# One DRAM store of a bias line becomes a short store and eight DRAM-to-DRAM copies

## The chip, the cores and the metric

The kernel runs on one core of a Trainium2 chip. The metric is the device time of one execution, in microseconds (us). The engines of the core are TensorE (PE; its weight loads PEld), VectorE (DVE), ScalarE (ACT), GpSimd (POOL) and SyncE (SP), which only issues transfers here. Transfers issued by SP and by ACT run on the same 16 DMA engines.

## What is computed

One step of a two-layer network over 576 tokens (512 of a prompt, 64 of a decoding request) with 1024 features. Layer 0 is a matrix-memory mixer and a gated FFN, layer 1 a differential attention with shared keys and values and a gated FFN. The change concerns the relative-position bias of the attention, which depends only on the distance between key and query:

```python
def _diff_attention(xm, k_all, v_all, q_offset, ...):
    table = rel_bias.astype(jnp.float32)          # 32 buckets x 8 heads
    def block(args):
        s = jnp.einsum('bqhcd,bkhcd->bhcqk', qblk, k_all)
        bias = table[_rel_bucket(k_pos[None, :] - q_pos[:, None])]
        p = jax.nn.softmax(jnp.where(mask, s + bias, NEG_BIG), axis=-1)
        a = p[:, :, 0] - lam * p[:, :, 1]
        return jnp.einsum('bhqk,bkhe->bqhe', a, v_all)
```

Because of that dependence, one line of 704 values for each head holds every bias that is needed: key minus query from -575 to 128. A tile of biases is a set of shifted windows of that line, one shift for each query.

## The kernel before, in words

The activations lie feature by token, 8 tiles of 128 features by 576 tokens. Every weight matrix is cut into units: a unit is 128x1024 values (512 KB), or 128x1408 for the down projections of the FFN. All projections are made in three matmuls each, with weights and activations split into a high and a low part. One unit goes through a fixed pipeline:

- SP loads it into `raw[u % 2]` (`load_unit`, L326 to L331). Before that it waits until POOL has split unit u-2 (`lo_split`).
- POOL makes `w_hi` and `w_lo` from it (`split_unit`, L408 to L418). It waits for the load and until TensorE has finished unit u-2 (`unit_done`).
- TensorE multiplies with it (`project`, L474 to L488: 8 k-tiles by 3 products by 2 halves of the tokens, 48 matmuls; `project_values`, L512 to L536: 30 matmuls of 512 columns a unit).

Beside the units SP loads tiles of the modulation weights, `ada_ring` (`load_ada`, L333 to L337, also 512 KB), which TensorE uses after a unit (L490 to L500). All of SP's loads go through one queue, q1 in the profile, in the order in which the code lists them. ACT's stores go through another, q10.

The order of units is: unit 0 the mixer's gates, 1 to 4 its queries, 5 to 8 its keys, 9 to 16 its values, then the rest of layer 0; 93 to 100 (`U_AK`) are the attention's keys, 101 to 108 (`U_AV`) its values, 109 to 116 its queries, 117 on (`U_AO`) its output projection. SP's loads for units 93 to 120 are the loop at L390 to L395; two tiles of `ada_ring` are loaded in it after units 94 and 96 (`KQ_ADA`, L83).

The bias line is made early. TensorE multiplies the bias table by one-hot columns (L562 to L566), VectorE copies the result to `line_sb`, 8 partitions by 704 values, and ACT stores it to DRAM (L996 and L997) as soon as it has prepared the first activations. The store writes the line of each head 128 times, so that DRAM holds 8 x 128 x 704 values. In layer 1, `load_head(h)` (L374 to L388) reads it back with a row step of LINE - 1, one value less than a row: row p of the tile is the line shifted by p. That gives `bias_p` (128 rows of 512 values) and `bias_s` (twice 64 rows of 576 values). `load_head(0)` is issued behind unit 117 and waits for the store (L378).

```python
sa.dma_start(line_dram, line_sb[:, :].unsqueeze(1).broadcast_to([H, P, LINE])).then_inc(line_stored, 16)   # L997
sp.wait_ge(line_stored, 16)                                                                                # L378
```

Of the kernel before, what the change touches and what calls it, by code (L numbers as in the profile page):

```python
# [37 lines left out]
P = 128  # L38
# [8 lines left out]
H = 8  # L47
# [7 lines left out]
LINE = 704  # L55
# [6 lines left out]
U_AK = U_FFN0 + 2 * FFN_HALF  # L62
U_AV, U_AQ, U_AO = U_AK + 8, U_AK + 16, U_AK + 24
# [8 lines left out]
def is_down(u):  # L72
    return any(d <= u < d + KT for d in down_units())


def stream_index(u):

    d = sum(1 for v in range(u) if is_down(v))
    return d if is_down(u) else u - d
# [41 lines left out]
def loop(eng, count, body, steps=None, per_turn=0):  # L121

    if count == 1:
        body(0)
        return
    start = steps.n if steps else 0
    with eng.Fori(0, count) as i:
        if steps:
            steps.turns = i * per_turn
        body(i)  # L130
    if steps:
        assert steps.n - start == per_turn, (steps.n - start, per_turn)
        steps.n, steps.turns = start + per_turn * count, 0


def build(nc, x_in, cond, consts, small, oh_line, table, w_stream, w_down, ada_w, c0n_in, kcache, vcache,
          line_dram, y_out, cp_out, cs_out, m_out, k_out, vp_out, vs_out):
    with ExitStack() as ctx:
        sem = lambda name: ctx.enter_context(nc.semaphore(name))
# [6 lines left out]
        def at(name, shape, offset, dt=F32):  # L146
            return nc.alloc_sbuf_tensor_at(name, shape, dt, offset=offset)
# [35 lines left out]
        line_sb = at("line_sb", [H, LINE], arena + 8 * T * 4)  # L183
# [51 lines left out]

        cond_ready, params_ready, x_ready, line_in = sem("cond_ready"), sem("params_ready"), sem("x_ready"), sem("line_in")
        line_stored, line_done, line_mm = sem("line_stored"), sem("line_done"), sem("line_mm")
        ada_first_in = [sem(f"ada_first_in{g}") for g in range(ADA_START // 2)]
        ada_in = [sem(f"ada_in{s}") for s in range(2)]
        ada_row_mm, ada_row_ready, xm_ready = (sem(n) for n in ("ada_row_mm", "ada_row_ready", "xm_ready"))  # L240
# [83 lines left out]
        @block.sync  # L324
        def _(sp):
            def load_unit(u0, i=0):  # L326

                src, blocks = (w_down, FH) if is_down(u0) else (w_stream, KT)
                if u0 >= 2:
                    sp.wait_ge(lo_split, i * 2 + (u0 - 1))  # L330
                sp.dma_start(raw[:, u0 % 2, 0:blocks * P], src[i * 2 + stream_index(u0)]).then_inc(raw_in[u0 % 2], 16)  # L331

            def load_ada(n0, i=0):  # L333

                if n0 >= ADA_START + 2:
                    sp.wait_ge(ada_mv, i * 2 + (n0 - ADA_START - 1))
                sp.dma_start(ada_ring[:, n0 % 2].rearrange("p k c -> p (k c)"), ada_w[i * 2 + n0]).then_inc(ada_in[n0 % 2], 16)  # L337

            def load_pairs(u0, pairs, ada0=None):

                def pair(i):
                    for j in range(2):
                        load_unit(u0 + j, i)
                        if ada0 is not None:
                            load_ada(ada0 + j, i)
                loop(sp, pairs, pair)

            sp.dma_start(cs_in, cond).then_inc(cond_ready, 16)
            for g in range(ADA_START // 2):
                dst = ada_first[0][:, 2 * g:2 * g + 2] if g < 6 else ada_first[1][:, 2 * g - 12:2 * g - 10]  # L350
                sp.dma_start(dst.rearrange("p u k c -> p u (k c)"),
                             ada_w[2 * g:2 * g + 2].rearrange("u p n -> p u n")).then_inc(ada_first_in[g], 16)
                if g == 1:
                    sp.dma_start(x[:, :, :], x_in).then_inc(x_ready, 16)
                    for c0, c1 in ((C_ID, C_MEAN + 1), (C_BLK, C_HEAD), (C_OHC, NCONST)):
                        sp.dma_start(cst[:, c0:c1], consts[:, c0:c1]).then_inc(params_ready, 16)
                    sp.dma_start(sml[:, :], small).then_inc(params_ready, 16)
            load_unit(0)
            load_unit(1)
            sp.dma_start(oh_sb[:, :], oh_line).then_inc(line_in, 16)  # L360
            sp.dma_start(tab_sb[:, :], table).then_inc(line_in, 16)
            sp.dma_start(c0n[:, :, :], c0n_in).then_inc(c0n_loaded, 16)
            load_ada(16)
            load_ada(17)
            for u in (2, 3, 4):
                load_unit(u)
            load_pairs(5, 25, 18)
            load_pairs(55, 1, 68)
            load_pairs(57, 3)
            load_pairs(63, 11, 70)  # L370
            load_pairs(85, 4)


            def load_head(h):  # L374
                s = h % 2
                if h == 0:
                    sp.wait_ge(ada_done, ADA_UNITS)
                    sp.wait_ge(line_stored, 16)  # L378
                elif h == 1:
                    sp.wait_ge(unit_done, U_AO)  # L380
                else:
                    sp.wait_ge(av_done, 5 * (h - 1))
                sp.dma_start(bias_p[s][:, :], bass.AP(line_dram.tensor, h * P * LINE + 191, [[LINE - 1, P], [1, 512]])).then_inc(stream_in[s], 16)
                for c in range(2):
                    sp.dma_start(bias_s[c * TS:(c + 1) * TS, s],
                                 bass.AP(line_dram.tensor, h * P * LINE + 63, [[LINE - 1, TS], [1, T]])).then_inc(stream_in[s], 16)
                sp.dma_start(kc_sb[s][:, :], kcache[h]).then_inc(stream_in[s], 16)
                sp.dma_start(vc_sb[s][:, :, :].rearrange("p k e -> p (k e)"), vcache[h]).then_inc(stream_in[s], 16)  # L388

            for u in range(U_AK, U_AO + 4):  # L390
                load_unit(u)
                if u in KQ_ADA:
                    load_ada(92 + KQ_ADA.index(u))
                if u == U_AO:
                    load_head(0)  # L395
            for h in range(1, H):
                load_head(h)
            load_pairs(U_AO + 4, 2)
            for hf in range(2):
                load_pairs(U_FFN1 + hf * FFN_HALF, FH)  # L400
                load_pairs(U_FFN1 + hf * FFN_HALF + 2 * FH, KT // 2)
# [531 lines left out]
        def _(sa):  # L933
# [60 lines left out]
                sa.wait_ge(xm_ready, m + 1)  # L994
                af(act[0][0][:, m, 0:T], xr[:, m, :], ACT.Copy).then_inc(hi_ready[A_IN], 1)
            sa.wait_ge(line_done, 2)  # L996
            sa.dma_start(line_dram, line_sb[:, :].unsqueeze(1).broadcast_to([H, P, LINE])).then_inc(line_stored, 16)  # L997


            sa.wait_ge(unit_done, 1)  # L1000
# [9 lines left out]
            for m in range(8):  # L1010
                u = U_Q + m
# [86 lines left out]
            for h in range(H):  # L1098
                u = U_O + h
# [790 lines left out]
```

## Time and profile before

| | |
|---|---|
| median of 3 runs | 1737.95 us (1737.13 to 1746.68) |
| the profiled execution | 1734.42 us, of it 1732.6 us in the span |
| mean granted TensorE clock | 0.972 |
| TensorE busy | 1639.4 us, 95% of the span |
| POOL, VectorE, ScalarE busy | 43%, 42%, 20% |
| q1, SP's loads | 46112 packets, 165.55 MB, 28.8% of 16 engines' span |
| q10, ACT's stores | 2728 packets, 10.49 MB, 2.5% |

The profile shows one execution. Busy times are shares of the whole span, so they hide short stretches in which another engine sets the pace; these are found in the views by window. The share of a DMA queue is the time that its packets took, as a share of the time of all 16 DMA engines.

### The profile page before, as it was taken

The numbers are of one execution on the slowest core, as the hardware profiler recorded it, in microseconds if no ns is written. First come the engines' busy times: TensorE is split into PE (matmuls) and PEld (weight loads), VectorE is DVE, ScalarE is ACT, GpSimd is POOL, SyncE is SP. The second block draws the span as 40 slices with busy tenths as digits, with TensorE's granted clock in tenths as the row PEclk, the third lists the DMA queues.
The fourth block names the chain that finished last, engine by engine and source line by source line (L and its number), as shares of the span: only waits on it lengthen the run. The fifth ranks groups of instructions, "written<-read, shape, count | busy, mean of one in ns | idle before, by whom it ended". The sixth has DMA issues, their size and how long they took to land.

```text
span 1732.6 us, 31223 instructions
## 1 busy us (share of the span) xinstructions
PE 1639.4 (95%) x12009; PEld 1479.1 (85%) x12009; DVE 719.1 (42%) x1230; ACT 354.8 (20%) x796; POOL 751.6 (43%) x436
## 2 busy tenths in 40 slices
PE   5789999999999999999999999788899999999999
PEld 2678733789999999999998879565799999999999
DVE  3400244545433321333586515678544443134431
ACT  2201034212211100111122112367521110001100
POOL 2534300234444554444554444224255555555563
PEclk8889999999999999999999999799899999999999
DMA  8364200234444422444322125222022222222231
GB/s 334 71 160 136 98 13 1 74 121 135 136 144 145 150 78 100 146 145 145 106 88 74 61 73 207 87 63 66 23 73 82 77 85 100 70 73 85 89 105 67
DMA packets 48908, 176.99 MB, mean 102 GB/s; under 512 B 5544, under 2 KB 5928, under 8 KB 48456
## 3 DMA queue, kind: packets, MB, share of 16 engines
q1 hardware_dynamic: 46112, 165.55, 28.8%
q10 hardware_dynamic: 2728, 10.49, 2.5%
q8 instruction: 47, 0.77, 0.2%
q14 instruction: 21, 0.17, 0.0%
HBM read 165.53 MB, written 10.49 MB: 102 GB/s over the span
## 4 chain that ended last, share of the span: by engine, by line
PE 83%; DVE 4%; DMA 3%; issue 2%; ACT 2%; POOL 1%; DVEq 0%; ACTq 0%; SPq 0%; POOLq 0%
PE psum L485 61%; PE psum L532 7%; PE psum L494 2%; DMA raw<-in_w_stream 2%; PE psum L653 1%; DMA ada_ring<-in_ada_w 1%; PE psum L635 1%; PE psum L654 1%; PE psum L876 1%; DVE act_lo L1368 1%; PE psum L919 1%; PE psum L779 1%; PE psum L863 1%; PE psum L505 1%; POOL w_lo L418 1%
## 5 line engine op out<-in xcount | busy, mean ns | idle before, releaser
L416 POOL TENSOR_SCALAR w_hi<-raw 128x1024 fp32r<-128x1024 f32 (+1 forms) x185 | 205.6, 1112 | 860.1 <-PE psum L485 672.7
L485 PE MATMUL psum<-act_hi,w_hi 128*128 128x288 f32 x2160 | 479.4, 303 | 19.9 <-POOL w_lo L418 10.6
L418 POOL TENSOR_TENSOR w_lo<-raw,w_hi 128x1024 fp32r<-128x1024 f32 (+1 forms) x185 | 487.8, 2637 | 15.4
L485 PE MATMUL psum<-act_lo,w_hi 128*128 128x288 f32 x2160 | 469.4, 299 | 0.0
L485 PE MATMUL psum<-act_hi,w_lo 128*128 128x288 f32 x2160 | 468.6, 298 | 0.0
L485 PEld LDWEIGHTS psum<-act_hi,w_hi 128*128 128x128 f32 x2160 | 351.7, 191 | 38.9 <-issue 31.2
L485 PEld LDWEIGHTS psum<-act_hi,w_lo 128*128 128x128 f32 x2160 | 353.1, 191 | 0.0
L485 PEld LDWEIGHTS psum<-act_lo,w_hi 128*128 128x128 f32 x2160 | 353.1, 191 | 0.0
L485 PE MATMUL psum<-hid_hi,w_hi 128*128 128x288 f32 x704 | 151.1, 296 | 0.0
L485 PE MATMUL psum<-hid_hi,w_lo 128*128 128x288 f32 x704 | 150.8, 296 | 0.0
L485 PE MATMUL psum<-hid_lo,w_hi 128*128 128x288 f32 x704 | 150.8, 296 | 0.0
L1411 DVE SCALAR_TENSOR_TENSOR tmp<-tmp,tiny 128x512 f32<-128x512 f32 x88 | 142.5, 1658 | 6.0 <-ACT tmp L1139 1.0
L1384 DVE SCALAR_TENSOR_TENSOR x<-psum,mod,x 128x288 f32 x144 | 51.2, 410 | 198.2 <-PE psum L485 194.5
L485 PEld LDWEIGHTS psum<-hid_hi,w_hi 128*128 128x128 f32 x704 | 113.4, 189 | 0.6 <-issue 0.6
L485 PEld LDWEIGHTS psum<-hid_hi,w_lo 128*128 128x128 f32 x704 | 113.5, 189 | 0.0
L485 PEld LDWEIGHTS psum<-hid_lo,w_hi 128*128 128x128 f32 x704 | 113.4, 189 | 0.0
L1406 DVE COPY tiny<-psum 128x2 f32<-128x2 f32 x44 | 7.0, 159 | 254.3 <-PE psum L485 254.3
L977 ACT ACTIVATE sml<-psum 128x128 f32<-128x128 f32 x80 | 22.3, 278 | 369.3 <-PE psum L494 368.9
L1145 ACT ACTIVATE hid_hi<-tmp 128x576 f32 (+1 forms) x44 | 30.2, 686 | 261.7 <-DVE tmp L1411 261.7
L1139 ACT ACTIVATE tmp<-tmp,tiny 128x512 f32<-128x512 f32 x88 | 42.3, 529 | 123.2 <-DVE tmp L1402 123.1
L532 PE MATMUL psum<-w_hi,act_hi 128*128 128x512 f32 x160 | 63.9, 399 | 3.8 <-DVE kf L1650 1.6
L532 PE MATMUL psum<-w_lo,act_hi 128*128 128x512 f32 x160 | 63.1, 395 | 0.0
(255 smaller groups left out, 1769.7 us busy)
## 6 DMA issues: line engine op xcount, KB each, us to landing
raw<-in_w_stream SPq DMA_DIRECT2D x153, 512.0 KB, 3.3
ada_ring<-in_ada_w SPq DMA_DIRECT2D x80, 512.0 KB, 3.3
raw<-in_w_down SPq DMA_DIRECT2D x32, 704.0 KB, 4.0
ada_first<-in_ada_w SPq DMA_DIRECT2D x8, 1024.0 KB, 15.2
line<-line_sb ACTq DMA_DIRECT2D x1, 2816.0 KB
x<-in_x SPq DMA_DIRECT2D x1, 2304.0 KB, 12.2
out_k<-kt_sb ACTq DMA_DIRECT2D x1, 2304.0 KB, 8.4
bias_s<-line SPq DMA_DIRECT2D x16, 144.0 KB, 3.4
```

The source lines that it names most:

```text
L416: pool.tensor_scalar(hi, src, 1.0, 0.0, ALU.mult, ALU.add).then_inc(hi_split, 1)
L418: pool.tensor_tensor(lo, src, hi.bitcast(F32), ALU.subtract).then_inc(lo_split, 1)
L485: last = mm(psum[:, 2 * s + half, 0:n_cols], w_parts[s][wp][:, k, :], parts[ap][:, k, half * HT:half * HT + n_cols], start=(k == 0 and n = ...
L494: last = mm(out(slice(32 * j, 32 * j + 32)), cs_col(2 * j + kk), w(2 * j + kk), start=(kk == 0), stop=(kk == 1))
L505: mm(psum[:, 5, bass.ds(i * 4 + 2 * n0, 2)], row_sb[:, n0 % 2, :], ada_sel, start=True, stop=True).then_inc(ada_done, 1)
L532: last = mm(psum[:, tt, :], parts[ap][:, k, t0:t0 + P], w, start=(k == 0 and n == 0), stop=(k == KT - 1 and n == 2))
L635: mm(psum[:, g % 2, 0:TP - j * P], k[:, j * P:(j + 1) * P], q[:, j * P:TP], start=True, stop=True).then_inc(s_ready, 1)
L977: af(row_sb[:, s, :], psum[:, row_bank(n0), 0:P], ACT.Copy).then_inc(row_ready, 1)
L1139: last = af(tmp[:, 4, a0:a1], tmp[:, 2, a0:a1], ACT.Silu, bias=shift_sb[:, 0, g:g + 1])
L1145: af(hid[0][:, i, :], tmp[:, 5, :], ACT.Copy).then_inc(hhi_ready, 1)
L1384: last = stt(out=xs, in0=psum[:, 2 * s + half, a0:a1], scalar=mod[:, i * 2 + (8 * c + j), g:g + 1], in1=xs, op0=ALU.mult, op1=ALU.add)
L1411: last = stt(out=tmp[:, 5, a0:a1], in0=tmp[:, 3, a0:a1], scalar=shift_sb[:, 1, g:g + 1], in1=tmp[:, 4, a0:a1], op0=ALU.add, op1=ALU.mult)
```

## The change

ACT stores only one row for each head (8 rows of 704 values). SP gets eight new transfers, one for each head, in the loop over the attention's units: `spread_line(h)` is issued right after the load of unit 93 + h, ahead of an `ada_ring` load where there is one. It copies row 0 of the head's block in DRAM to the block's rows 1 to 127. The first of them waits for ACT's store. `load_head(0)` waits for all eight.

```diff
+        line_spread = sem("line_spread")
...
                 if h == 0:
                     sp.wait_ge(ada_done, ADA_UNITS)
-                    sp.wait_ge(line_stored, 16)
+                    sp.wait_ge(line_spread, 16 * H)
...
+            def spread_line(h):
+
+                if h == 0:
+                    sp.wait_ge(line_stored, 16)
+                sp.dma_start(line_dram[h, 1:P, :], line_dram[h, 0:1, :].broadcast_to([P - 1, LINE])).then_inc(line_spread, 16)
+
             for u in range(U_AK, U_AO + 4):
                 load_unit(u)
+                if u < U_AV:
+                    spread_line(u - U_AK)
                 if u in KQ_ADA:
                     load_ada(92 + KQ_ADA.index(u))
...
             sa.wait_ge(line_done, 2)
-            sa.dma_start(line_dram, line_sb[:, :].unsqueeze(1).broadcast_to([H, P, LINE])).then_inc(line_stored, 16)
+            sa.dma_start(line_dram[:, 0, :], line_sb[:, :]).then_inc(line_stored, 16)
```

## Rows read from the trace of the kernel before

**Rows 1.** The page: busy time, share and instructions; the chain that ended last.

```profile
PE 1639.4 (95%) x12009; PEld 1479.1 (85%) x12009; DVE 719.1 (42%) x1230; ACT 354.8 (20%) x796; POOL 751.6 (43%) x436
...
PE 83%; DVE 4%; DMA 3%; issue 2%; ACT 2%; POOL 1%; DVEq 0%; ACTq 0%; SPq 0%; POOLq 0%
```

**Rows 2.** Busy time by stretch: window, us, busy (instructions), clock, DMA share, GB/s.

```profile
60.00:80.00 20.00, 19.48 (x170) 18.83 (x168) 10.26 (x9) 6.64 (x10) 6.66 (x4) 1.00 0.62 99
80.00:100.00 20.00, 13.71 (x101) 13.43 (x101) 0.00 (x0) 0.93 (x2) 6.80 (x4) 0.83 0.63 121
100.00:120.00 20.00, 11.41 (x100) 10.74 (x98) 0.00 (x0) 1.46 (x3) 6.82 (x4) 0.83 0.63 154
120.00:140.00 20.00, 19.86 (x161) 18.37 (x156) 1.01 (x8) 3.27 (x9) 10.32 (x6) 1.00 0.56 182
```

**Rows 3.** The waits from 79 to 135 us: total us, times, longest.

```profile
POOL w_hi L416 <- DMA raw<-in_w_stream: 36.7, 5, 16.3
...
PE psum L494 <- DMA ada_ring<-in_ada_w: 8.6, 1, 8.6
...
PE psum L485 <- POOL w_lo L418: 6.8, 1, 6.8
```

**Rows 4.** The chain, 78 to 136 us: start, duration, what.

```profile
110.72 1.08 PE psum L494 x16
111.80 7.63 PE psum L485 x48
...
120.12 6.60 PE psum L485 x48
...
127.41 6.60 PE psum L485 x48
134.01 0.02 issue
134.03 0.66 ACT qk L1013
```

**Rows 5.** TensorE's timeline, end of unit 3 and start of unit 4.

```profile
79.19 0.29 PE L494 MATMUL psum<-ada_ring,cst 128*32 128x128 f32 x3
...
86.27 0.84 PE L485 MATMUL psum<-act_hi,w_hi 128*128 128x288 f32 x2 [6.79 <-POOL w_lo L418]
```

**Rows 6.** Queue q10 from 66.5 to 69.5 us: packets, MB, share of 16 engines.

```profile
q10 hardware_dynamic: 56, 0.16, 48.5%
```

**Rows 7.** Median us to landing of a unit's load, 60 to 100 us; the whole span.

```profile
raw<-in_w_stream SPq DMA_DIRECT2D x4, 512.0 KB, 20.0
...
raw<-in_w_stream SPq DMA_DIRECT2D x153, 512.0 KB, 3.3
```

**Rows 8.** Queue q1 from 940 to 950 us, where one 512 KB load runs.

```profile
DMA packets 144, 0.52 MB, mean 52 GB/s; under 512 B 16, under 2 KB 16, under 8 KB 144
...
q1 hardware_dynamic: 144, 0.52, 16.7%
```

**Rows 9.** SP's timeline, 881 to 925 us: the last is the load of unit 97.

```profile
889.91 9.12 SPq L331 DMA_DIRECT2D raw<-in_w_stream  x2
899.07 0.43 SPq L337 DMA_DIRECT2D ada_ring<-in_ada_w  x1
...
924.90 0.33 SPq L331 DMA_DIRECT2D raw<-in_w_stream  x1
```

**Rows 10.** The chain in the key projection: units 97, 98; the first values unit.

```profile
946.56 6.42 PE psum L485 x48
...
953.96 6.42 PE psum L485 x48
...
977.75 7.42 PE psum L532 x31
```

**Rows 11.** POOL's timeline, the split of unit 97.

```profile
938.40 1.05 POOL L416 TENSOR_SCALAR w_hi<-raw 128x1024 fp32r<-128x1024 f32 x1 [3.87 <-PE psum L485]
939.53 2.40 POOL L418 TENSOR_TENSOR w_lo<-raw,w_hi 128x1024 fp32r<-128x1024 f32 x1
```

**Rows 12.** Queue q1, 1111 to 1119 us; queue q10, 1060 to 1070 us.

```profile
q1 hardware_dynamic: 736, 1.61, 68.8%
...
q10 hardware_dynamic: 263, 2.78, 66.0%
```

**Rows 13.** The page's DMA issues: the store that is changed.

```profile
line<-line_sb ACTq DMA_DIRECT2D x1, 2816.0 KB
```

## Prediction

> **What bounds the kernel now.** I read the page first: TensorE is busy for 95% of the span and makes 83% of the chain that ended last [rows 1]. So a change to transfers pays only where TensorE waits for one, and costs only where it makes TensorE wait. Next I read the busy time by stretch around the store of the bias line, which ACT issues at about 58.6 us. From 60 to 80 us TensorE is busy, from 80 to 120 us it is busy for 25.1 of 40 us while the DMA engines are busy for 0.63 of the time at a modest rate, from 120 us it is busy again [rows 2]. The waits say what was late: POOL waited 36.7 us for units, TensorE 8.6 us for an `ada_ring` tile and 6.8 us for a split that POOL began late [rows 3]. Then I looked at the store by itself. From 66.5 to 69.5 us only its queue runs: 56 packets in 3 us, 48.5% of 16 engines, so 7.8 engines busy; 0.485 x 16 x 3 / 56 = 0.416 us for a packet of 2816 B [rows 6]. The store has 8 rows (the heads) as its outermost count, and it keeps 8 engines busy. It holds 8 x 128 packets, 128 for each engine, 53 us of work at that pace. Beside it a unit's load lands after 20.0 us instead of 3.3 [rows 7], because half of its packets go through the eight engines that the store keeps busy.
>
> **Part 1: the store shrinks from 2816 KB [rows 13] to 22.5 KB.** Eight packets take the place of 1024, so units 4 to 8 should arrive as later units do. Unit 3 with its modulation ends at 79.48 us [rows 5]. Undisturbed, a unit costs 7.29 us from start to start (120.12 to 127.41) and 6.60 us alone [rows 4]. Units 4 to 8 then end at 79.48 + 4 x 7.29 + 6.60 = 115.2 us; they ended at 134.0. **Gain: 18.8 us.** The waits give the same: 6.8 + 8.6 us, and the slow restarts behind them, in which the clock fell to the lower of its two levels, 1.2 GHz, for a few us (granted 0.83 on average in these stretches [rows 2]), account for the other 3.4. What is late next is nothing: from 120 us on, with the same loads and no store, TensorE is at 19.86 of 20 us. ACT's issue of the store sits ahead of the gates' evacuation, but TensorE does not wait for that from 60 to 80 us, so I count nothing for it.
>
> **Part 2: eight copies in q1 beside units 93 to 100.** Each is 127 rows of 2816 B, 357.6 KB, and 127 packets. The question that decides the case is on how many engines they run. A load of 128 rows makes 144 packets, 9 for each engine, one of them small [rows 8]; the store of 8 rows kept 8 engines busy. Every transfer seen is dealt out in equal shares of its outermost count. 127 is a prime number: equal shares leave **one engine with all 127 packets**. The Trainium skill says this outright: in "DMA: Bandwidth & Descriptors", section "Why a DMA increments its semaphore by 16 and not by 1", the number of engines is the largest up to 16 that divides the outermost count on both sides, and 127 partitions run on one. By that rule the sum is the one below; the trace agrees for 8 and 128, and has no odd count to show.
>
> *One copy on one engine.* No row shows a DRAM-to-DRAM packet. The nearest rows that read DRAM in rows of this size are the head loads (2048 and 2304 B rows): 0.688 x 16 x 8 us = 88.1 engine-us for 1.61 MB, 18.3 GB/s for an engine [rows 12]. That gives 0.154 us a packet and **C = 19.6 us** a copy, which I take: both ends are in DRAM, and rows of 2 to 3 KB are the right size. The low bound is ACT's large stores to DRAM, 0.66 x 16 x 10 = 105.6 engine-us for 2.78 MB, 26.3 GB/s, C = 13.6 [rows 12]. The high bound is the store's own 0.416 us, C = 52.8 [rows 6]; it reads the same few partitions over and over, which the copy does not, so I think it far off. The same page, in "Latency and other measured facts", has 207 GB/s each way for copies between DRAM tensors on all engines; as an estimate that is 12.9 GB/s an engine, C = 27.6, and by it the execution would take 1873 us.
>
> *What waits behind them.* A unit's load has 8 packets and a small one on that same engine, in the same queue and in order, and its wait in POOL is for all of it. A load of 512 KB takes 0.167 x 10 = 1.67 us of each engine [rows 8]. The load of unit 93 is issued at 889.91 us [rows 9] and takes 3.3 us [rows 7], so the first copy starts at 893.2. Until unit 101 has landed, the engine must do 8 copies, 8 loads (units 94 to 101) and 2 `ada_ring` tiles. With C at 13.6 or above it is never empty: unit 97 was requested at 924.90 us [rows 9], when the engine would already be four requests behind. So unit 101 lands at 893.2 + 10 x 1.67 + 8C = 909.9 + 8C. POOL splits it in 3.5 us [rows 11], and TensorE starts it at 913.4 + 8C. It started at 977.75 [rows 10]. With 1.5 us for one slow restart (the second one of part 1: 7.63 + 1.08 us where the usual is 6.60 and about 0.6 [rows 4]) the delay is 8C - 62.9 us. **Loss: 156.8 - 62.9 = 93.9 us.** The 62.9 us are the cover: between unit 97 and unit 98 TensorE works 7.4 us [rows 10] and an engine needs only 1.67 of them for a load, and a load is some 10 us early for POOL (unit 97: 924.90 + 3.3 against a split that begins at 938.40 [rows 11]). With C at 19.6 a unit takes 21 us instead of 7.4.
>
> SP is in order, so an issue of a copy stands ahead of the next load; but the next load waits for POOL anyway, and the time is below the spare. The wait of the first copy for `line_stored` costs nothing: that store is over by some 800 us. The wait in `load_head(0)` now is for the copies, which end ahead of unit 101's load, over 100 us before it. The amount that is read back is the same. Nothing later gives the delay back, since all stages behind hang on TensorE.
>
> **Sum.** Against the profiled execution: 1734.4 - 18.8 + 93.9 = 1809.5 us. That execution is 3.5 us under the median of the runs shown, so **1813 us**. By C = 13.6: 1734.4 - 18.8 + 45.9 = 1761.5, or 1765 as a median. By C = 52.8: 1734.4 - 18.8 + 359.5 = 2075.
>
> **Rivals.**
> - *The copies run on all 16 engines* (shares rounded up, 8 packets for each engine, 1.2 us at 0.154). For it: no row shows a count that doesn't divide. Against it: both counts that rows show went in equal shares. Then a load lands at most 1.2 us later, with 10 us spare, and only part 1 is left: 1734.4 - 18.8 = 1715.6, as a median **1719 us**, faster. Chance 0.12. Seen from the price, it decides below C = 10.2 us (8C = 62.9 + 18.8), 0.080 us a packet; on one engine that is 35 GB/s, which no row reaches (chance 0.02, about no change).
> - *The copies crawl*: one engine, and a packet costs more than 0.24 us, because each reads the same 2816 B again and writes DRAM behind it. For it: the store, which also reads the same source over and over, took 0.416 us. Against it: the head loads. From 1900 to 2075 us. Chance 0.08.
> - *The front doesn't speed up*: the loads of units 4 to 8 were late for another reason. Against it: a queue with 48.5% of the engines in the very stretch [rows 6]. Then 1813 + 19 = 1832 us. Chance 0.03.
>
> **The numbers.** The forecast, one engine at 0.107 to 0.24 us a packet, has 0.75. That and the third rival lie in 1765 to 1900, about 0.78. I keep the range there: the fast case at 1719 and the slow tail are what it leaves out. A measurement of this kernel tells about 0.5%, 9 us, from no change. Faster 0.12, within it 0.02, slower 0.86.
>
> **What would show it.** Right: from 80 to 120 us TensorE busy all through and units landing after 3.3 us; from about 930 to 1070 us TensorE in bursts of 6.4 us at intervals of 21, POOL waiting for `raw`, DMA engines busy for little more than a sixteenth of the time, the copies about 20 us or more from issue to landing, the first values unit starting near 1050 us (977.75 - 18.8 + 93.9). Wrong: the copies landing within some 4 us and the key projection as before (the first rival); intervals above 32 us (the second); 20 us landings before 120 us (the third).

## The result and the profile after

The changed kernel takes 1763.62 us (1763.06 to 1766.38, 4 runs) against 1737.62 us (1737.13 to 1746.68, 4 runs): 1.014 times as long, 95% interval 1.0106 to 1.0175. It is slower, as forecast, but by 26 us and not by 75; that is just below the range. The profiled execution took 1763.78 us, 29.4 more than the one of before.

**The front.** The view by stretch, with the columns of [rows 2], and the landing of a unit's load from 60 to 100 us:

```profile
80.00:100.00 20.00, 20.00 (x174) 19.54 (x174) 0.00 (x0) 2.05 (x5) 9.67 (x6) 1.00 0.47 151
100.00:120.00 20.00, 19.86 (x174) 18.50 (x173) 1.01 (x8) 3.80 (x9) 10.32 (x6) 1.00 0.40 137
```

```profile
raw<-in_w_stream SPq DMA_DIRECT2D x6, 512.0 KB, 3.3
```

TensorE works for 39.86 of 40 us where it worked for 25.1 [rows 2], and a load lands after 3.3 us where it took 20.0 [rows 7]. The first matmul of the mixer's core starts at 200.0 us and no longer at 218.4: 18.4 us gained, 18.8 forecast.

**The key projection.** The queue from 963 to 970 us, when only a copy runs:

```profile
q1 hardware_dynamic: 65, 0.18, 6.5%
```

6.5% of 16 engines is 1.04 engines: one engine carries the copy. 65 packets in 7 us are 0.108 us for each. The forecast had 0.154. POOL's timeline, its splits of units 96 and 98 to 100 (the `ada_ring` tile behind unit 96's copy makes the step at unit 97, not shown, 1.3 us longer):

```profile
925.22 1.04 POOL L425 TENSOR_SCALAR w_hi<-raw 128x1024 fp32r<-128x1024 f32 x1 [10.80 <-DMA raw<-in_w_stream]
...
956.50 1.58 POOL L425 TENSOR_SCALAR w_hi<-raw 128x1024 fp32r<-128x1024 f32 x1 [10.95 <-DMA raw<-in_w_stream]
...
971.47 1.05 POOL L425 TENSOR_SCALAR w_hi<-raw 128x1024 fp32r<-128x1024 f32 x1 [10.60 <-DMA raw<-in_w_stream]
...
986.47 1.04 POOL L425 TENSOR_SCALAR w_hi<-raw 128x1024 fp32r<-128x1024 f32 x1 [10.96 <-DMA raw<-in_w_stream]
```

Units come 15.0 us apart, where TensorE needs 7.4. SP's timeline in the same stretch, the load of unit 98, its copy, the load of unit 99:

```profile
930.69 14.22 SPq L332 DMA_DIRECT2D raw<-in_w_stream  x1
944.95 0.86 SPq L395 DMA_DIRECT2D line<-line  x1
945.85 13.95 SPq L332 DMA_DIRECT2D raw<-in_w_stream  x1
```

The issue of a load is itself held for 14 us while the engine that carries the copies is behind. That engine is called engine 0 below; the views don't number the engines. The first matmul of the attention's scores starts at 1135.7 us and not at 1105.6. From the 10 small matmuls behind unit 93 (L815, now L824) to there it takes 227.6 us and not 182.5: the copies cost 45.1 us. They were to cost 93.9.

The rest of the account: of the 18.4 us of the front 15.0 are left when unit 93 ends. The mixer's core took 89.1 us from its first to its last score matmul where it took 85.9; TensorE's granted clock was 0.92 in that stretch where it was 0.96. The kernel below that keeps the long store has 89.3 there too, so the short store is not what lengthens it. -15.0 + 45.1 = 30.1, and 29.4 remain at the end.

### The profile page after: what moved, and what is told of

Its sections match the earlier page's. It is cut to its first block, busy times and chain, and to the rows that moved or that the text cites. A ratio compares the mean times of both kernels' runs of the same rounds, so it can differ in the third digit from the quotient of the medians.

```text
span 1762.0 us, 31231 instructions
## 1 busy us (share of the span) xinstructions
PE 1647.7 (94%) x12009; PEld 1484.5 (84%) x12009; DVE 735.9 (42%) x1230; ACT 354.9 (20%) x796; POOL 756.3 (43%) x436
## 4 chain that ended last, share of the span: by engine, by line
PE 84%; DMA 3%; SPq 3%; ACT 2%; DVE 2%; POOL 2%; issue 1%; POOLq 0%; DVEq 0%; ACTq 0%
PE psum L494 63%; PE psum L541 7%; DMA raw<-in_w_stream 3%; PE psum L503 3%; SPq L332 2%; PE psum L662 1%; PE psum L644 1%; PE psum L663 1%; SPq L338 1%; PE psum L885 1%; PE psum L928 1%; POOL w_lo L427 1%; PE psum L872 1%; PE psum L514 1%; PE psum L900 1%
## 5 line engine op out<-in xcount | busy, mean ns | idle before, releaser
L541 PE MATMUL psum<-w_hi,act_lo 128*128 128x512 f32 x160 | 64.0, 400 | 0.0
```

The lines of the kernel that those rows point to most:

```text
L541: last = mm(psum[:, tt, :], parts[ap][:, k, t0:t0 + P], w, start=(k == 0 and n == 0), stop=(k == KT - 1 and n == 2))
```

## The experiments

Theory 1: a DMA is dealt out in equal shares of its outermost count, so 127 rows stand on one engine, and each load in the same queue waits behind them there. Theory 2: SP's issue of the copies costs the time. Theory 3: the bytes of the copies disturb the loads. "Keys" below is the time from the end of unit 93 to the first score matmul (182.5 us before, 227.6 in the changed kernel). All kernels start from the changed one. Where the number of copies or stores differs, the counts that are waited for are changed with it; the cuts of the code leave that out, and `...` stands for the rest of a line.

**rows112_15.** 112 + 15 rows.

```diff
-                sp.dma_start(line_dram[h, 1:P, :], ...broadcast_to([P - 1, LINE])).then_inc(line_spread, 16)
+                for r0, r1 in ((1, 113), (113, P)):
+                    sp.dma_start(line_dram[h, r0:r1, :], ...broadcast_to([r1 - r0, LINE])).then_inc(line_spread, 16)
```

> Each head's copy is cut into two: 112 rows and 15 rows. Theory 1 (equal shares of the rows; a load stands behind the copy on engine 0): 7 packets on each of 16 engines and 1 on each of 15, under 1 us beside each load, no wait for a unit in the key projection. Only the gain of the short store is left: 1738 - 19 = 1719 us. Theory 2 (SP's issue of the copies is what costs, whatever the engines): 16 issues in place of 8, the key projection as slow as in the changed kernel or slower, 1764 us or more. Theory 3 (the DRAM traffic of the copies disturbs the loads): the same bytes, 1764 us.

Measured: 1722.65 us, ratio 0.9897 (0.9861 to 0.9934). In the key projection POOL waits for no load any more, only for TensorE:

```profile
POOL w_hi L426 <- PE psum L495: 58.5, 13, 9.9
```

Keys: 185.5 us. The same bytes, issued by the same SP in twice the number of issues, cost at most 3 us. Even these are not the issues: rows125_2 below has as many and takes 182.2 us. TensorE is busy in all of the first 20 us of this stretch in both, but with a granted clock of 0.82 here and 1.00 there. Theories 2 and 3 are out.

**rows97_30 and rows67_60.** The same edit with the cut at row 98 or at row 68.

> Each head's copy is cut into 97 rows (a prime, one engine) and 30 rows (15 engines, 2 packets each). Theory 1, set to the changed kernel (0.111 us a packet, delay 46.6 us at 127 packets): 8 x (30 x 0.111 - 0.22) = 25 us less on engine 0, delay 22 us, so 1738 - 19 + 22 = 1741 us. Units land about 11.9 us apart (15.0 in the changed kernel). Theories 2 and 3: 1764 us or more.

Measured: 1737.91 us, ratio 0.9993 (0.9975 to 1.0012). Its POOL timeline:

```profile
954.84 1.04 POOL L426 TENSOR_SCALAR w_hi<-raw 128x1024 fp32r<-128x1024 f32 x1 [8.10 <-DMA raw<-in_w_stream]
966.77 1.04 POOL L426 TENSOR_SCALAR w_hi<-raw 128x1024 fp32r<-128x1024 f32 x1 [8.46 <-DMA raw<-in_w_stream]
978.78 1.04 POOL L426 TENSOR_SCALAR w_hi<-raw 128x1024 fp32r<-128x1024 f32 x1 [8.09 <-DMA raw<-in_w_stream]
```

Units come 12.0 us apart. Engine 0 has 97 + 2 packets for each and not 127: 28 packets less for 3.0 us less, so 0.107 us a packet and 15.0 - 127 x 0.107 = 1.4 us for a load. Keys: 202.0 us, 19.5 over before; 22 were expected.

> Each head's copy is cut into 67 rows (a prime, one engine) and 60 rows (15 engines, 4 packets each). Theory 1: engine 0 needs 67 x 0.111 + 0.44 + about 1 for the load = 8.9 us a unit against the 7.4 of TensorE; 8 x 1.5 = 12 us are lost, which the early start of the loads (11 to 15 us) covers. Delay 0 to 2 us, so 1719 to 1721 us, though one engine still carries half of every copy. Theories 2 and 3: 1764 us or more.

Measured: 1719.54 us, ratio 0.9898 (0.986 to 0.9936), keys 182.7 us. One engine still carries 67 + 4 of the 127 packets of each copy, and nothing waits. What counts is only whether the busiest engine keeps up long enough: 127, 99 and 71 packets cost 45.1, 19.5 and 0.2 us.

**rows125_2.** The cut at row 126.

> Each head's copy is cut into 125 rows and 2 rows. Equal shares: 125 = 5 x 25, five engines with 25 packets (2.7 us), two with 1. While only a copy runs, 5 of 16 engines are busy, a share of 0.31, and the key projection doesn't wait. If shares were rounded (or one engine taken for every odd count), the share would be 1.0 for 0.9 us, or 0.06 for 14 us.

One execution took 1723.41 us. The queue from 884 to 886 us:

```profile
q1 hardware_dynamic: 88, 0.25, 31.8%
```

0.318 x 16 = 5.1 engines for 125 = 5 x 25 rows, at 0.114 us a packet. Shares are equal, and the largest divisor up to 16 decides: 5 of 125, 1 of 127. It is one execution, so only the count of engines is read from it, not its time.

**every_third.** The copies behind units 93, 96, ... 114.

```diff
-                if u < U_AV:
-                    spread_line(u - U_AK)
+                if u < U_AO and (u - U_AK) % 3 == 0:
+                    spread_line((u - U_AK) // 3)
```

> The eight copies keep their 127 rows and their queue, but stand behind every third unit (93, 96, ... 114), through the key, value and query projections. Theory 1: engine 0 needs 14 us for a copy and 3 x 1.3 us for the loads in the 22 us that TensorE takes for three units, and the one load behind a copy is late by less than its 15 us of cover. No delay, 1719 us, with one engine still carrying every copy. If a copy on one engine cost its own time wherever it stands, the delay would be that of the changed kernel, 1764 us.

Measured: 1730.85 us, ratio 0.9954 (0.9931 to 0.9977), keys 194.8 us: 12 us of loss, none expected. POOL's timeline, the split of unit 114 and of unit 115:

```profile
1062.13 1.05 POOL L425 TENSOR_SCALAR w_hi<-raw 128x1024 fp32r<-128x1024 f32 x1 [10.15 <-DMA raw<-in_w_stream]
...
1077.38 1.05 POOL L425 TENSOR_SCALAR w_hi<-raw 128x1024 fp32r<-128x1024 f32 x1 [11.77 <-DMA raw<-in_w_stream]
```

The first seven copies are hidden: TensorE never waits for a split before 1055 us. The eighth stands behind unit 114. SP's timeline there, an `ada_ring` tile, the load of unit 114, the copy, the load of unit 115:

```profile
1057.32 0.33 SPq L338 DMA_DIRECT2D ada_ring<-in_ada_w  x1
1057.69 0.47 SPq L332 DMA_DIRECT2D raw<-in_w_stream  x1
1058.20 0.58 SPq L395 DMA_DIRECT2D line<-line  x1
1058.82 6.39 SPq L332 DMA_DIRECT2D raw<-in_w_stream  x1
```

`KQ_ADA` has four entries and not only the two named in the description of the kernel: tiles are loaded after units 94, 96, 112 and 113. SP is in order, and the last tile waited 14.9 us for TensorE to be done with an older one, with unit 114's load behind it. That load was late before the change too (issued at 1067.80 us, 0.37 us after the tile; POOL waited 10.2 us). So this copy starts with no cover left: unit 115's load lands 18.4 us after its issue, and TensorE waits 8.0 us for the splits where it waited 0.8. These are 7 of the 12 us. The rest is a lower granted clock at both ends, 0.85 in the first 20 us of the stretch (1.00 before) and 0.89 from 1055 to 1105 us (0.97 for the same work before). The theory stands; the expectation took the cover to be the same everywhere.

**act_queue.** The same 127-row copies, issued by ACT in its own stream, one with every second unit of the mixer's projections.

```diff
+                if m % 2 == 1:
+                    spread_line(m // 2)
...
+                    if n == 1:
+                        spread_line(4 + 2 * nh)
...
+                spread_line(5 + 2 * nh)
```

> The eight 127-row copies, unchanged in shape, are issued by ACT in its own queue, one with every second unit of the mixer's query, key and value projections (every 15 us). Theory 1 in its strict form (what costs is the order within SP's queue, not the engine's load): engine 0 takes turns between the two queues, a unit's load lands 1 to 3 us later than 3.3 us, no wait, 1719 us. If the engine's total work were the cause: each pair of units puts 14.1 us of copy and some 4 us of loads on engine 0 in 15 us, 8 x 3 = 24 us less the cover, 1725 to 1735 us.

Measured: 1736.68 us, ratio 0.9975 (0.9957 to 0.9993), nearly 18 us above the 1719 that theory 1 gave and within 2 us of the 1725 to 1735 of its rival. Keys: 184.5 us. Where the copies run, a unit's load lands after 6.0 us (median from 60 to 200 us) and not 3.3, and from 60 to 120 us TensorE waits for none: in another queue a long copy delays the loads on its engine by 3 us and does not block them. But from 120 to 140 us TensorE is busy for 11.08 of 20 us. ACT's timeline says why:

```profile
116.01 7.46 ACTq L1004 DMA_DIRECT2D line<-line  x1
...
123.55 16.16 ACTq L1030 DMA_DIRECT2D out_m<-rows  x1
```

ACT itself was held for 24 us at issuing, as SP is in the changed kernel, and ACT has evacuations to do. TensorE waited for them:

```profile
PE psum L507 <- ACT sml L979: 9.8, 1, 9.8
```

A third hold of 6.1 us follows at 192 us, and TensorE waits 3.4 us behind it. These two waits are 13 us; the slower clock around them (granted 0.83 from 140 to 160 us, 0.86 from 180 to 200) is the likely rest, not taken apart. The rival expectation, engine 0's total work, is not what delays: no unit was late. But that work, 13.7 us for a copy and the loads beside it every 15 us, may be what held ACT.

**old_store_and_copies.** The long store kept, with the copies.

```diff
-            sa.dma_start(line_dram[:, 0, :], line_sb[:, :]).then_inc(line_stored, 16)
+            sa.dma_start(line_dram, line_sb[:, :].unsqueeze(1).broadcast_to([H, P, LINE])).then_inc(line_stored, 16)
```

> The long store of before is kept beside the new copies, which write the same values again: part 2 of the change without part 1. Expected are the front as before and the key projection as in the changed kernel: 1738 + 46.6 = 1785 us. If the short store gained nothing, it would be the changed kernel's 1764.

Measured: 1784.0 us, ratio 1.0267 (1.0216 to 1.0318). Keys: 228 us. The front is as before (TensorE busy for 25.4 of 40 us) and the keys are as in the changed kernel, so the two parts of the change add up: 1784.0 - 1763.6 = 20.4 us are what the short store gains.

**unaligned.** The reads start 4 bytes further.

```diff
-                sp.dma_start(line_dram[h, 1:P, :], line_dram[h, 0:1, :]...
+                sp.dma_start(line_dram[h, 1:P, 0:LINE - 1], line_dram[h, 0:1, 1:LINE]...
```

> Each copy reads its row from the second value on, at an address 4 bytes further, and writes 703 values (the biases are shifted by one place: this part of the result is changed). It asks why the head loads, whose rows start at every 4-byte step, moved 18.3 GB/s an engine and misled the forecast, while the copies move 26. If the start address is the cause, a packet costs 0.154 us and units land 20.9 us apart: 8 x 5.9 = 47 us more, 1811 us. If one more piece of 256 B is read for each packet, 12 in place of 11: units 16.2 us apart, about 1773 us. If the address does not matter: 1764 us.

Measured: 1763.59 us, ratio 1.015 (1.0098 to 1.0201). Units come 14.98 us apart, as in the changed kernel. A start 4 bytes on costs nothing here. The dearer case of the expectation, one more piece of 256 B, was not made: the read is 4 bytes shorter as well and ends where the row ends, so with a row that starts on a boundary of 256 B it touches the same 11 pieces.

**half_packets.**

```diff
+                for c0 in (0, LINE // 2):
+                    sp.dma_start(line_dram[h, 1:P, c0:c0 + LINE // 2], ...
```

> Each copy is cut by columns into two of 127 packets of 1408 B, both on one engine: the same bytes in twice the packets. If the cost goes by bytes (26 GB/s): units land 15.0 us apart as in the changed kernel, 1764 us. If a packet has a fixed part of 0.02 us: 17.5 us apart, 1784 us. If the shorter rows of the head loads (2048 and 2304 B) explain their slower pace, the fixed part must be about 0.15 us: over 30 us apart, 1880 us or more.

Measured: 1771.85 us, ratio 1.02 (1.0148 to 1.0253). Units come 16.2 us apart (979.75 to 995.91 in POOL's timeline): 127 packets more for 1.2 us, a fixed part of 0.009 us. Shorter rows explain little of the head loads' pace.

**one_copy.** One copy for all heads, behind unit 93's load.

```diff
-                sp.dma_start(line_dram[h, 1:P, :], line_dram[h, 0:1, :].broadcast_to([P - 1, LINE])).then_inc(line_spread, 16)
+                sp.dma_start(line_dram[:, 1:P, :], line_dram[:, 0:1, :].broadcast_to([H, P - 1, LINE])).then_inc(line_spread, 16)
...
-                if u < U_AV:
+                if u == U_AK:
```

> One copy for all heads (8 x 127 rows) behind unit 93's load, in place of eight. Equal shares of its outermost count, 8, put 127 packets on each of 8 engines, as the old store had 128. If a packet between two DRAM places costs the 0.108 us of the changed kernel on all 8 engines, they are busy for 14 us once, one load is late by less than its 15 us of cover, and only part 1 is left: 1719 us. If 8 engines at once make the packets as slow as the old store's (0.416 us), they are busy for 53 us: 53 - 15 = 38 us late, 1757 us.

Measured: 1720.86 us, ratio 0.9892 (0.9864 to 0.992). The queue from 882 to 885 us:

```profile
q1 hardware_dynamic: 211, 0.59, 51.3%
```

Eight engines at 8 x 3 / 211 = 0.114 us a packet, 198 GB/s, where the old store had eight engines at 0.416 us. So neither the number of engines nor writing to DRAM made that store slow. Keys: 182.7 us, nothing lost.

**store_four_heads.** Heads 0 to 3 by the long store, the others by copies of 112 and 15 rows.

```diff
+            sa.dma_start(line_dram[4:H, 0, :], line_sb[4:H, :]).then_inc(line_stored, 16)
+            sa.dma_start(line_dram[0:4], line_sb[0:4, :].unsqueeze(1).broadcast_to([4, P, LINE])).then_inc(line_stored, 16)
```

> It asks what made a packet of the old store cost 0.416 us. ACT stores the lines of heads 0 to 3 128 times as before, from 4 partitions and on 4 engines; heads 4 to 7 get one row and copies of 112 and 15 rows. If reading from a few partitions is the limit (the 8 partitions gave 52.6 GB/s in all), 4 partitions give half of it, a packet stays at about 0.42 us, 4 engines are held for 53 us, and the front is as slow as before: 1738 us. If the 8 engines slowed each other elsewhere, a packet falls to about 0.21 us, 27 us, and some 14 of the 19 us are gained: 1724 us.

Measured: 1738.04 us, ratio 0.999 (0.9971 to 1.0009). The queue from 66.5 to 69.5 us, to be set beside [rows 6]:

```profile
q10 hardware_dynamic: 28, 0.08, 24.3%
```

Four engines, half of the packets in the same 3 us, so 0.43 us for a packet as before. Half of the bytes hold half of the engines for the same time, and the front is as slow: TensorE busy for 26.5 of 40 us between 80 and 120 us. A unit's load lands after 19.2 us although only a quarter of it goes through busy engines: what counts is the slowest engine. So the limit is on the reading side: 4 partitions gave 28 x 2816 B in 3 us, 26 GB/s, 8 gave 52.6. In both stores each engine reads one partition over and over, so the runs don't tell a limit of the partitions together from one of each engine's rereading. Loads of units were in flight in part of this window, in their own queue.

## Why the prediction failed

**Right: part 1.** 18.8 us forecast, 18.4 in the trace and 20.4 between two kernels that differ by it alone. The reason was right too, loads behind busy engines; that it was half of each load did not matter, as four busy engines made the front as slow (store_four_heads).

**Right: one engine for 127 rows.** 1.04 engines in the trace, and 5.1 for 125 rows. The rule of the Trainium skill ("DMA: Bandwidth & Descriptors", "Why a DMA increments its semaphore by 16 and not by 1") holds for every count whose engines were read here: 4, 8, 125 and 127.

**Right: queue, cover and its size.** The form 8C - 62.9 us needs correction only for a load, which costs 1.4 us of a busy engine and not 1.67; with ten loads that is 2.7 us. With C = 127 x 0.108 = 13.7 it gives 46.7, and 44 with the lighter load; 45.1 were measured. Had C been 13.7, the forecast would have read 1737.6 - 18.8 + 46.7 = 1765.5 us.

**Wrong: the value taken for C.** The step that failed is "the nearest rows that read DRAM in rows of this size are the head loads", 0.154 us a packet, C = 19.6. The copy ran at 0.108, C = 13.7, which is the row that I had put down as the low bound (ACT's large stores, 26.3 GB/s for an engine, 13.6). Multiplied by eight copies, 5.9 us are 47 us, nearly all of the miss of 49. The likeness in row size was the wrong guide: half as long packets add 0.009 us each, and a start 4 bytes on nothing.

The row was also misread. Of the 1.61 MB in the window of [rows 12], 0.52 MB are the load of unit 117, and as much are the first head's keys and values; only 0.56 MB are read from the bias line. All of them are loads into SBUF, of 64 or 128 rows, and the unit's load, with rows of 4096 B, goes at 0.52 MB in 26.7 engine-us [rows 8], 19.6 GB/s for an engine. So 18 to 20 GB/s is what loads into SBUF with rows of 2 to 4 KB show, and nothing in that row spoke for a copy between two places in DRAM. Part of it is the way of counting: a 512 KB load is 1.67 us of each engine by its share [rows 8], and 1.4 us by the intervals when the engine is backed up. Why such loads are slower for an engine than the copy stays open: SBUF as the destination and 16 engines at once are both candidates. An estimate for the copy on 16 engines (rows112_15, the share of a copy and a load less 26.7 engine-us for the load) gives 0.133 us a packet in one window and 0.093 in another, too coarse to decide.

**Wrong: the range.** It ended at C = 13.6 and a median of before 3.5 us above the profiled execution. That put its low end on a bound of one term, with nothing left for the spread of the medians, and the term fell on the bound. The Trainium skill's 207 GB/s each way for copies between DRAM tensors ("DMA: Bandwidth & Descriptors", "Latency and other measured facts") was measured with rows of 16 KiB. My estimate from it, 12.9 GB/s for one engine of 16, does not carry over: one engine moved 26 GB/s here, and eight moved 198 together.

**Incomplete: the issue.** I wrote that the issue of a copy costs less than the spare. SP was held for 12 to 14 us at a load behind a copy. As far as the trace shows it cost nothing of its own: a copy and a load (13.7 + 1.3 us) fill the 15.0 us between units, so the load would have waited in the queue instead. On ACT such holds led to 13 us of waits in TensorE.

## What to carry to other kernels

Give every DMA an outermost count with a large divisor up to 16: cutting 127 rows into 112 and 15, or taking the heads as outermost dimension of one copy, turned 1.4% slower into about 1% faster. A transfer that sits on few engines is harmless until those engines fall behind what is queued on them: add up packets on the busiest engine, against the time that the consumer leaves, and look for places where the requests come late anyway (unit 114), since there is no cover there. For an engine's own pace take rows in which it never stops and in which nothing else runs, and look at the queue that issues: whoever issues into a backed-up engine is held as well.

## What the runs showed of the hardware beyond that

- A store in which each engine reads one partition over and over is slow: 0.416 us for 2816 B from 8 partitions on 8 engines, 0.43 from 4 partitions on 4 engines, against 0.114 on 8 engines when the source is DRAM.
- A DMA's issue can take 14 us on SP and 16 us on ACT (usually 0.3 to 0.9) when an engine that it needs is far behind. For the load issued at 930.69 us the landings give, as an estimate, some 220 packets ahead of it on engine 0 when the hold began and some 95 when it ended.
- One engine copies between two places in DRAM at 26 GB/s in packets of 2816 B, from the start of the row and from 4 bytes on; at 1408 B it needs 8% longer for a unit's copy and load together (16.2 us against 15.0).
